# The FoX head beside each GDN head placed half a head later in a hybrid decoder step

## Chip, cores and metric

The kernel runs on one core of a Trainium2 chip. The metric is the device time of one execution in microseconds, as the median of three runs.

## What is computed

One layer of a hybrid decoder for 512 prompt tokens behind 16 meta tokens and for 8 sequences of 4 sampled tokens. A GDN group (gated delta rule, 8 heads) and a FoX group (softmax attention with a forget gate, 8 heads) run on one combined projection; a PEER layer, which looks up single neurons as experts, follows. Cut to what matters:

```python
xn = rmsnorm(h); p = xn @ w_in                      # columns: GDN q|k|v, a, b, z, FoX q|k|v, f, og
# GDN: conv + SiLU on q|k|v, L2 norm of q and k, then per chunk of tokens
rhs = beta * (v - exp(G) * (k @ S)); u = triangular_solve(a_strict, rhs)
o = exp(G) * (q @ S) + (qk * decay) @ u;  S = exp(G_last) * S + (k * tail).T @ u
gdn = rmsnorm(o) * silu(z)
# FoX: QK norm, causal softmax(q k / sqrt(128) + c_t - c_s) v; sampled tokens also see a paged cache
fox = rmsnorm(o_fox) * sigmoid(og)
h = h + concat(gdn, fox) @ w_out
# PEER: 8 heads x 16 experts of 16384 for each token
idx, gate = top16(product keys); hid = gelu(x . expert_u[idx]); h = h + sum(gate * hid * expert_v[idx])
```

## The kernel before

The 560 rows (32 sampled, 16 meta, 512 prompt) are worked in two groups: **a** has the first 256 rows (two tiles of 128, the sampled and meta rows in the first), **b** the other 304 (tiles of 128, 128 and 48). `front` runs for each group the stages norm and gates, `heads`, the output product, the norm before PEER, and the routing. Between two stages all engines meet at a barrier, and a stage's queue programs wait for its last stores before they get there. The experts of a group are gathered from memory (128 rows of 8 KB each by one indirect DMA from the POOL queue, into a ring of five buffers) and used by DVE, one item for each gather: a dot product (L1812) or a weighted sum (L1825). The gathers of group a begin with group b: in b's `heads` 330 items are placed between its own work (`quota`), and what is left runs at the end. Group a has no items.

`heads` is where the change lies. Each head pair needs eight segments of the projection, each 128 columns wide and 16 matmuls long (L795, `segment`, three or two PSUM buffers `pj`), with its 1 MB weight tile loaded by SP (L693); group a also stores each tile, packed, for group b (L1133). ACT takes a finished segment out of PSUM (`evacuations`, L1118 for the raw rows of GDN's q, k and v, L1124 for FoX's, L1127 for the gate z, L1130 for og).

The order of work on every engine is set by marks. The programs of GDN, FoX, projections, evacuations and items are generators that yield a number ahead of each step, and `Marks` always emits the step with the lowest number. A head is 100 marks long; GDN head h and FoX head h both begin at mark 100h, and the steps in them are at fixed distances (`at + 15` and so on). The projections are placed by

```python
G_Q, G_K, G_V, F_Q, F_K, F_V, G_Z, F_OG = range(8)

def segment_mark(j, step):
    return 12.5 * (j - 6) + 12.5 * step / KT
```

so six segments come ahead of mark 0 and the last ends at mark 725. Items stand at 100 * HEADS * (i + 0.5) / quota. An engine works strictly in this order; between engines, semaphores say when a result is there.

The steps of a GDN head that the text speaks of: at 2.5 DVE waits for the evacuated q, k, v rows (L1343); from 3 to 9 it does the convolution (L1356, L1358); at 12 SiLU (L1367); at 15 PE sums the squares (L844, L848); at 16 to 18.5 root and inverse on ACT, then the scaling on DVE (L1385); at 20 PE turns k (L859); from 28 to 76 six levels of the triangular solve go to and fro between PE and DVE (L886, L892, L896, L1413, L1417, L1421); from 77 to 97 one round for each tile carries the state S on; at 98 the output norm (ACT L1195, DVE L1462, L1463), at 98.6 PE turns it (L951), at 99 DVE writes mixT (L1467). In a the state of the sampled rows is stored by POOL at 98 (L1598), in b the final state by SP at 99 (L739). The steps of a FoX head: norms from 1 to 9 (L1025, L1038), in a the sampled rows against the cache from 9 to 37 (page transposes L967 with copies L1501 and L1234, products L985 and L1010), then the prompt blocks (scores L1063, exponential L1250, transposes L1080, products L1086, L1544), at 89 to 94 the output norm, its turn (L1095) and mixT (L1562).

## Time and profile before

| | us |
|---|---|
| three runs | 4745.6, 4751.4, 4766.0 (median 4751.4) |
| profiled execution, its own time | 4779.3 |
| its span | 4777.5 |
| busy: DVE, PE, POOL, ACT | 3371.8, 2412.1, 2363.8, 542.1 |
| `heads` of group a, first projection to last mixT | 68 to 936 |
| `heads` of group b, first projection to last mixT | 1351 to 2476 |
| bytes moved by DMA | 1515 MB, mean 317 GB/s |

PE is the matrix engine (PEld its weight loads), DVE the vector engine, ACT the scalar engine, POOL the one that issues the gathers, SP the one that issues the weight loads. Busy time is the time with an instruction in execution; the granted clock of PE is shown as a share of its full speed. "Idle before" is the time that an engine stood still ahead of a group of instructions, with what ended it. The `heads` stages of the two groups are read apart, since their limits differ.

### The profile page before, as it was taken

Reading aid. Unit: us, or ns where it says so; the run is one execution under the profiler, and the core shown is the slowest. Engines: PE = TensorE matmul, PEld = TensorE weight load, DVE = VectorE, ACT = ScalarE, POOL = GpSimd, SP = SyncE. Lnnn points to the kernel's source line nnn. Section 1 sums busy time; section 2 is a strip of 40 time slices with the busy share of each in tenths; the row PEclk is TensorE's granted clock in tenths of the full one; section 3 lists DMA queues with packets and bytes.
Section 4 is the critical chain, followed back from the end, with each engine's and each line's share of the span. In section 5 each row is a group of like instructions: output and inputs, shape, how many; then the busy total and the mean of one; then the engine's idle time right before and its main releaser. Section 6 shows DMA issues by size and latency. Waiting matters only on the chain. (4 is left out here: it accounts for less than half of the span.)

```text
span 4777.5 us, 35023 instructions
## 1 busy us (share of the span) xinstructions
PE 2412.1 (50%) x11665; PEld 1922.4 (40%) x11665; DVE 3371.8 (71%) x4421; ACT 542.1 (11%) x1305; POOL 2363.8 (49%) x1222
## 2 busy tenths in 40 slices
PE   5999999797388888888749465100000000000000
PEld 5888888686366666665537343100000000000000
DVE  1332333306748899988876678889988988979998
ACT  1222222201122222222210000000000000000000
POOL 1100000000125665656564312288887877878886
PEclk8988999798789999999859787555555555555555
DMA  6756666277659999999988855499999999999998
GB/s 181 216 175 197 196 204 190 74 279 242 220 195 413 393 396 394 393 380 392 343 345 350 326 219 202 147 397 420 404 393 394 422 390 409 422 369 421 408 421 354
DMA packets 444012, 1515.01 MB, mean 317 GB/s; under 512 B 42092, under 2 KB 276256, under 8 KB 277896
## 3 DMA queue, kind: packets, MB, share of 16 engines
q0 software_dynamic: 162080, 1160.16, 60.7%
q1 hardware_dynamic: 269080, 251.94, 16.9%
q10 hardware_dynamic: 12672, 100.67, 5.2%
q8 instruction: 93, 1.52, 0.1%
q14 instruction: 87, 0.71, 0.0%
HBM read 1384.96 MB, written 127.53 MB: 317 GB/s over the span
## 5 line engine op out<-in xcount | busy, mean ns | idle before, releaser
L1812 DVE CUSTOM_DVE_ANT_0 ex_ring<-ex_ring,ex_xi 128x2048 f32<-128x2048 f32 x544 | 1244.4, 2289 | 145.0 <-DMA ex_ring<-in_peer_u_dram,idx_all 77.2
L1825 DVE SCALAR_TENSOR_TENSOR ex_y<-ex_ring,ex_wt,ex_y 128x2048 f32<-128x2048 f32 x538 | 1264.4, 2350 | 113.9 <-DMA ex_ring<-in_peer_v_dram,idx_all 72.8
L1760 POOL DMA_INDIRECT ex_ring<-in_peer_u_dram,idx_all x384 | 790.2, 2058 | 342.8 <-DVE ex_hid L1812 135.1
L1760 POOL DMA_INDIRECT ex_ring<-in_peer_v_dram,idx_all x384 | 826.9, 2153 | 224.3 <-DVE ex_hid L1812 118.9
L795 PE MATMUL heads_b_pj<-xnT_b,heads_b_w 128*128 128x304 f32 x2048 | 608.0, 436 | 11.8 <-DMA heads_b_w<-w_scratch 8.5
L795 PE MATMUL heads_a_pj<-xnT_a,heads_a_w 128*128 128x256 f32 x2048 | 534.2, 401 | 20.5 <-DMA heads_a_w<-in_w_in_dram 20.5
L1760 POOL DMA_INDIRECT ex_ring<-in_peer_v_dram,ex_idx_s x160 | 310.7, 1942 | 328.8 <-DVE ex_hid L1812 156.6
L795 PEld LDWEIGHTS heads_b_pj<-xnT_b,heads_b_w 128*128 128x128 f32 x2048 | 380.5, 198 | 123.2 <-issue 15.3
L1760 POOL DMA_INDIRECT ex_ring<-in_peer_u_dram,ex_idx_s x160 | 320.6, 2004 | 207.9 <-DVE ex_y L1825 135.0
L795 PEld LDWEIGHTS heads_a_pj<-xnT_a,heads_a_w 128*128 128x128 f32 x2048 | 386.7, 201 | 72.4 <-DMA heads_a_w<-in_w_in_dram 21.1
L1592 POOL TENSOR_TENSOR heads_a_ub<-heads_a_uN,const 128x1024 f32<-128x1024 f32 x8 | 15.2, 1895 | 490.6 <-ACT heads_a_uN L1186 490.6
L1784 ACT ACTIVATE ex_act<-ex_hid 128x16 f32<-128x16 f32 x34 | 7.3, 215 | 1831.2 <-DVE ex_hid L1812 1831.1
L1756 POOL DMA_DIRECT2D ex_xi<-xi_scratch x13 | 6.9, 549 | 405.4 <-POOLq L249 330.5
L1892 PE MATMUL out_b_acc<-out_b_w,mixT_b 128*128 128x256 f32 (+1 forms) x768 | 170.3, 383 | 30.4 <-DMA out_b_w<-w_out_scratch 30.4
L1892 PEld LDWEIGHTS out_b_acc<-out_b_w,mixT_b 128*128 128x128 f32 (+1 forms) x768 | 128.8, 169 | 71.6 <-DMA out_b_w<-w_out_scratch 30.6
L2061 PE MATMUL route_b_pq<-mixT_b,route_b_w 128*128 128x304 f32 x512 | 143.0, 443 | 21.9 <-DMA route_b_w<-w_q_scratch 21.9
L2061 PEld LDWEIGHTS route_b_pq<-mixT_b,route_b_w 128*128 128x128 f32 x512 | 102.8, 203 | 60.8 <-DMA route_b_w<-w_q_scratch 22.1
L1892 PE MATMUL out_a_acc<-out_a_w,mixT_a 128*128 128x256 f32 x512 | 112.8, 384 | 25.9 <-DMA out_a_w<-in_w_out_dram 25.9
L2061 PE MATMUL route_a_pq<-mixT_a,route_a_w 128*128 128x256 f32 x512 | 114.6, 385 | 7.5 <-DMA route_a_w<-in_peer_w_query_dram 7.5
L1417 DVE TENSOR_TENSOR heads_a_yX<-heads_a_yX,heads_a_R 128x256 f32<-128x256 f32 x48 | 20.2, 421 | 136.0 <-PE heads_a_R L892 136.0
L1892 PEld LDWEIGHTS out_a_acc<-out_a_w,mixT_a 128*128 128x128 f32 x512 | 98.6, 193 | 39.9 <-DMA out_a_w<-in_w_out_dram 26.1
L2061 PEld LDWEIGHTS route_a_pq<-mixT_a,route_a_w 128*128 128x128 f32 x512 | 98.7, 194 | 21.4 <-DMA route_a_w<-in_peer_w_query_dram 7.9
(552 smaller groups left out, 3471.4 us busy)
## 6 DMA issues: line engine op xcount, KB each, us to landing
heads_a_w<-in_w_in_dram SPq DMA_DIRECT2D x64, 1024.0 KB, 6.1
w_scratch<-heads_a_w ACTq DMA_DIRECT2D x64, 1024.0 KB, 4.5
heads_b_w<-w_scratch SPq DMA_DIRECT2D x64, 1024.0 KB, 8.8
out_a_w<-in_w_out_dram SPq DMA_DIRECT2D x8, 2048.0 KB, 8.6
w_out_scratch<-out_a_w ACTq DMA_DIRECT2D x8, 2048.0 KB, 6.4
route_a_w<-in_peer_w_query_dram SPq DMA_DIRECT2D x16, 1024.0 KB, 7.1
w_q_scratch<-route_a_w ACTq DMA_DIRECT2D x16, 1024.0 KB, 6.7
out_b_w<-w_out_scratch SPq DMA_DIRECT2D x8, 2048.0 KB, 11.9
```

Of the source, the lines that this page charges most:

```text
L795: last = nc.tensor.matmul(pj[j % PJ][:, 0:N], B.w[:, j % W, k, :], xnT[:, k, :], start=(k == 0), stop=(k == KT - 1))
L1417: nc.vector.tensor_tensor(wide(B.XT), wide(B.XT), R1[:, 0:TW], ALU.subtract).then_inc(sem["XT_ready"], 1)
L1592: nc.gpsimd.tensor_tensor(B.ub[:], B.uN[:, 0, :].unsqueeze(1).to_broadcast([P, NB, HD]), cst("members", 0, NB).unsqueeze(2).to_broadcast([ ...
L1756: pool.dma_start(self.xi[part.on, :], self.xi_rows[part.xi_rows]).then_inc(self.sem["xi_in"], 16)
L1760: pool.indirect_dma_start(self.ring[:, i % RING, :], None, self.tables[which], bass.IndirectOffsetOnAxis(ap=self.index(s, g, k), axis=0)). ...
L1784: self.nc.scalar.activation(self.act[:, g % 2, :], self.hid[:, g % 2, :], ACT.Gelu).then_inc(self.sem["activated"], 1)
L1812: nc.vector.tensor_tensor_reduce(ring, ring, self.xi[:], 1.0, 0.0, ALU.mult, ALU.add, self.hid[:, g % 2, k:k + 1]).then_inc(self.sem["cons ...
L1825: nc.vector.scalar_tensor_tensor(y, ring, wt, y, ALU.mult, ALU.add).then_inc(self.sem["consumed"], 1)
L1892: last = nc.tensor.matmul(acc[0:b - a, i, 0:GW], mixT[:, k, a:b], w[:, c % 2, k, :], start=(k == 0), stop=(k == KT - 1))
L2061: last = nc.tensor.matmul(pq[s][:, 0:N], B.w[:, slot, k, :], xiT[:, k, :], start=(k == 0), stop=(k == KT - 1))
```

## The change

FoX head h begins at mark 100h + 50 instead of 100h, on all engines and in both groups. The segments are put in another order, z ahead of FoX's q, k and v, and all segments come three places later against the GDN heads: three of them ahead of mark 0 instead of six. The items of group b are spread over 850 marks instead of 800. The loads of the cache pages go with the FoX head.

```diff
-G_Q, G_K, G_V, F_Q, F_K, F_V, G_Z, F_OG = range(8)
-BASES = (0, C_K, C_V, C_FQ, C_FQ + HEADS * HD, C_FQ + 2 * HEADS * HD, C_Z, C_OG)
+G_Q, G_K, G_V, G_Z, F_Q, F_K, F_V, F_OG = range(8)
+BASES = (0, C_K, C_V, C_Z, C_FQ, C_FQ + HEADS * HD, C_FQ + 2 * HEADS * HD, C_OG)
...
 def segment_mark(j, step):
-    return 12.5 * (j - 6) + 12.5 * step / KT
+    return 12.5 * (j - 3) + 12.5 * step / KT
+
+
+def fox_mark(h):
+
+    return 100.0 * h + 50
...
-                            yield 100.0 * (h - 1) + step + 0.5 * i
+                            yield fox_mark(h - 1) + step + 0.5 * i
...
-                    at, n = 100.0 * h, h + 1
+                    at, n = fox_mark(h), h + 1
...
-                    at, n, qkv = 100.0 * h, h + 1, B.f_qkvT[:, h % 2]
+                    at, n, qkv = fox_mark(h), h + 1, B.f_qkvT[:, h % 2]
...
-                    yield 100.0 * HEADS * (i + 0.5) / quota
+                    yield (100.0 * HEADS + 50) * (i + 0.5) / quota
```

The new kernel's lines are five higher from here on (L795 is L800, L844 is L849, L1467 is L1472). What the marks make of it is seen in the order of the instructions. First PE in group a, early in a GDN head, from the transposes of the conv rows (L838, then L843) to the two sums of squares (L844 and L848, then L849 and L853). Before:

```order
L838 MATMUL heads_a_R<-const,heads_a_rowc 24x128 x3
L1030 MATMUL heads_a_F<-const,heads_a_f_qkvT 128x128 x2
L1032 MATMUL heads_a_F<-const,heads_a_f_qkvT 96x128
L795 MATMUL heads_a_pj<-xnT_a,heads_a_w 128x256 x2
L1038 MATMUL heads_a_F<-const,heads_a_f_qkvT 128x128 x2
L795 MATMUL heads_a_pj<-xnT_a,heads_a_w 128x256 x3
L967 MATMUL heads_a_F<-const,heads_a_kc 128x128 x8
L795 MATMUL heads_a_pj<-xnT_a,heads_a_w 128x256 x4
L967 MATMUL heads_a_F<-const,heads_a_kc 128x128 x8
L795 MATMUL heads_a_pj<-xnT_a,heads_a_w 128x256 x4
L844 MATMUL heads_a_R<-heads_a_qke,const 128x256
L848 MATMUL heads_a_R<-heads_a_qke,const 128x256
```

and now, on to the transposes of k (L864, before L859):

```order
L843 MATMUL heads_a_R<-const,heads_a_rowc 24x128 x3
L800 MATMUL heads_a_pj<-xnT_a,heads_a_w 128x256 x5
L1091 MATMUL heads_a_F<-heads_a_vM,heads_a_PT 128x128
L800 MATMUL heads_a_pj<-xnT_a,heads_a_w 128x256 x8
L849 MATMUL heads_a_R<-heads_a_qke,const 128x256
L853 MATMUL heads_a_R<-heads_a_qke,const 128x256
L800 MATMUL heads_a_pj<-xnT_a,heads_a_w 128x256 x2
L858 MATMUL heads_a_R<-const,heads_a_qkvT 128x128 x2
L800 MATMUL heads_a_pj<-xnT_a,heads_a_w 128x256 x4
L864 MATMUL heads_a_R<-const,heads_a_qkvT 128x128 x2
```

The projections are as many; the FoX matmuls between them have gone to the other half of the head, and one product of the FoX head before (L1091) stands there.

Second DVE at the end of group b's `heads`, from the last GDN head's mixT on. Before, the stage ended with it (the branches are the border of the stage):

```order
L1812 ISA ex_ring,ex_hid<-ex_ring,ex_xi 128x2048
L1812 ISA ex_hid 128x1
L1462 RECIPROCAL heads_b_ors<-heads_b_ort 128x3
L1463 TENSOR_TENSOR heads_b_gU<-heads_b_R,heads_b_ors 128x384
L1825 SCALAR_TENSOR_TENSOR ex_y<-ex_ring,ex_wt,ex_y 128x2048
L1467 SCALAR_TENSOR_TENSOR mixT_b<-heads_b_R,vecs,heads_b_gz 128x304
L679 UNCONDITIONAL_BRANCH
L1907 UNCONDITIONAL_BRANCH
```

and now 20 items follow, with the second half of the last FoX head between them; the first rows are:

```order
L1472 SCALAR_TENSOR_TENSOR mixT_b<-heads_b_R,vecs,heads_b_gz 128x304
L1817 ISA ex_ring,ex_hid<-ex_ring,ex_xi 128x2048
L1817 ISA ex_hid 128x1
L1830 SCALAR_TENSOR_TENSOR ex_y<-ex_ring,ex_wt,ex_y 128x2048
L1545 RECIPROCAL heads_b_rec<-heads_b_den 128x1
L1817 ISA ex_ring,ex_hid<-ex_ring,ex_xi 128x2048
L1817 ISA ex_hid 128x1
L1830 SCALAR_TENSOR_TENSOR ex_y<-ex_ring,ex_wt,ex_y 128x2048
```

The items there were taken out of the heads before, which now have fewer each.

## Rows read from the trace of the kernel before

**Rows 1.** Stretches: us, then busy us (instructions) per engine, granted clock, DMA share, GB/s

```profile
core 0: us, PE busy (x) PEld busy (x) DVE busy (x) ACT busy (x) POOL busy (x), PEclk, DMA share, GB/s
68.00:886.00 818.00, 799.54 (x4352) 693.85 (x4353) 253.79 (x734) 198.35 (x497) 77.00 (x86) 0.92 0.65 198
886.00:936.00 50.00, 41.03 (x194) 34.03 (x192) 17.21 (x45) 6.23 (x23) 2.84 (x2) 0.69 0.05 22
1360.00:1400.00 40.00, 40.00 (x158) 29.71 (x157) 4.75 (x9) 2.07 (x5) 0.93 (x1) 1.00 0.52 180
1535.00:2300.00 765.00, 651.09 (x3089) 474.92 (x3087) 693.72 (x767) 186.48 (x410) 479.11 (x238) 0.95 0.98 392
2388.00:2476.00 88.00, 47.60 (x196) 37.59 (x194) 85.23 (x87) 11.73 (x36) 71.42 (x31) 0.56 0.93 362
```

**Rows 2.** Waits of DVE, 1350 to 1534 us: total us, times, longest

```profile
DVE heads_b_rowc L1343 <- ACT heads_b_raw L1118: 21.9, 1, 21.9
```

**Rows 3.** Waits of PE in group a, 62 to 936 us

```profile
PE heads_a_F L967 <- DVE heads_a_kc L1501: 8.2, 8, 1.0
```

**Rows 4.** Timeline, third GDN head of group a: start us, us, engine, line, operation

```profile
321.86 0.44 PE L951 MATMUL heads_a_R<-const,heads_a_gU 128*128 128x128 f32 x2 [0.99 <-DVE heads_a_gU L1463]
...
324.67 1.27 DVE L1356 TENSOR_SCALAR heads_a_yX<-heads_a_raw,heads_a_tap 128x224 f32<-128x224 f32 x6
...
336.11 0.61 DVE L1358 SCALAR_TENSOR_TENSOR heads_a_yX<-heads_a_raw,heads_a_tap,heads_a_yX 128x224 f32<-128x224 f32 x2
...
339.59 0.59 PE L844 MATMUL heads_a_R<-heads_a_qke,const 128*128 128x256 f32 x2
...
343.91 0.69 DVE L1385 TENSOR_TENSOR heads_a_qkvT<-heads_a_qkvT,heads_a_th_root 128x512 f32<-128x512 f32 x1 [3.93 <-ACT heads_a_th_root L1167]
```

**Rows 5.** Groups of instructions by line: busy us, mean ns | idle before, releaser

```profile
L795 PE MATMUL heads_a_pj<-xnT_a,heads_a_w 128*128 128x256 f32 x2048 | 534.2, 401 | 20.5 <-DMA heads_a_w<-in_w_in_dram 20.5
L967 PE MATMUL heads_a_F<-const,heads_a_kc 128*128 128x128 f32 x128 | 18.3, 276 | 8.2 <-DVE heads_a_kc L1501 8.2
L1025 PE MATMUL heads_a_F<-heads_a_f_root,const 128*128 128x256 f32 x32 | 8.2, 379 | 0.0
L1358 DVE SCALAR_TENSOR_TENSOR heads_a_yX<-heads_a_raw,heads_a_tap,heads_a_yX 128x224 f32<-128x224 f32 (+1 forms) x144 | 53.7, 437 | 0.6
L1356 DVE TENSOR_SCALAR heads_a_yX<-heads_a_raw,heads_a_tap 128x224 f32<-128x224 f32 (+1 forms) x48 | 10.1, 283 | 0.0
```

**Rows 6.** A table load by line, and the root of a GDN head with its reader

```profile
L1140 ACT ACT_TABLE_LOAD x16 | 20.5, 1283 | 0.3
...
317.26 0.30 ACT L1195 ACTIVATE heads_a_ort<-heads_a_oms,const 128x2 f32<-128x2 f32 x1
...
321.19 0.16 DVE L1462 RECIPROCAL heads_a_ors<-heads_a_ort 128x2 f32<-128x2 f32 x1
```

**Rows 7.** The GDN heads' mixT, line L1467: ns min/median/max, first and last start

```profile
L1467 DVE SCALAR_TENSOR_TENSOR mixT_a<-heads_a_R,vecs,heads_a_gz x8: 483/484/485, 216.4 to 935.5; 128x256 f32<-128x256 f32 x8
L1467 DVE SCALAR_TENSOR_TENSOR mixT_b<-heads_b_R,vecs,heads_b_gz x8: 526/530/534, 1533.8 to 2475.2; 128x304 f32<-128x304 f32 x8
```

**Rows 8.** The items of the experts on DVE, groups by line

```profile
L1812 DVE CUSTOM_DVE_ANT_0 ex_ring<-ex_ring,ex_xi 128x2048 f32<-128x2048 f32 x544 | 1244.4, 2289 | 145.0 <-DMA ex_ring<-in_peer_u_dram,idx_all 77.2
L1825 DVE SCALAR_TENSOR_TENSOR ex_y<-ex_ring,ex_wt,ex_y 128x2048 f32<-128x2048 f32 x538 | 1264.4, 2350 | 113.9 <-DMA ex_ring<-in_peer_v_dram,idx_all 72.8
```

**Rows 9.** Timeline at the end of both `heads` stages

```profile
935.50 0.48 DVE L1467 SCALAR_TENSOR_TENSOR mixT_a<-heads_a_R,vecs,heads_a_gz 128x256 f32<-128x256 f32 x1 [0.53 <-PE heads_a_R L951]
945.76 0.33 SPq L1872 DMA_DIRECT2D hres_a<-in_x_sample_dram  x1
...
2475.16 0.53 DVE L1467 SCALAR_TENSOR_TENSOR mixT_b<-heads_b_R,vecs,heads_b_gz 128x304 f32<-128x304 f32 x1
...
2489.59 1.30 SPq L1872 DMA_DIRECT2D hres_b<-in_x_prompt_dram  x3
```

**Rows 10.** DMA issues: count, KB each, median us from issue to landing

```profile
out_gdn_sample_dram<-heads_a_sout POOLq DMA_DIRECT2D x8, 512.0 KB, 6.1
...
out_gdn_prompt_dram<-heads_b_S SPq DMA_DIRECT2D x8, 64.0 KB, 12.5
```

More of the change, by code:

```diff
@@ L1206, in fox @@
                 for h in range(HEADS):
-                    at, n, qkv = 100.0 * h, h + 1, B.f_qkvT[:, h % 2]
+                    at, n, qkv = fox_mark(h), h + 1, B.f_qkvT[:, h % 2]
                     yield at + 1
@@ L1284, in item_mark @@
             def item_mark(i):
-                return 100.0 * HEADS * (i + 0.5) / quota
+                return (100.0 * HEADS + 50) * (i + 0.5) / quota
             act.wait_ge(sem["f_cleared"], 5)
@@ L1483, in fox @@
                 for h in range(HEADS):
-                    at, n, qkv = 100.0 * h, h + 1, B.f_qkvT[:, h % 2]
+                    at, n, qkv = fox_mark(h), h + 1, B.f_qkvT[:, h % 2]
                     order = Counter(dve, sem["f_order"], n, 20)
@@ L1601, in fox @@
                 for h in range(HEADS):
-                    at, n = 100.0 * h, h + 1
+                    at, n = fox_mark(h), h + 1
                     yield at + 10
```

## The prediction

> **What bounds the kernel now.** I read the stage windows first, because the two groups have different limits. In group a (68 to 886 us) PE is busy 799.5 of 818 us while DVE is busy 254 and the DMA engines at 0.65 [rows 1]: PE alone sets the pace. After the last projection, from 886 to 936 us, PE is busy 41 of 50 us at a granted clock of 0.69, so 9 us are latency and part of the rest is the low clock. In group b, from 1535 to 2300 us, the DMA engines are at 0.98 and DVE busy 694 of 765 us, PE only 651 [rows 1]: the expert gathers and the DVE work on them set the pace. Just ahead, from 1360 to 1400 us, the reverse holds: PE projects without a gap at full clock, DVE has 4.8 us of work and the DMA engines stand at 0.52. That stretch is the lead in which six segments are projected before head 0 begins, and DVE spends 21.9 us of it waiting for the evacuated raw tile [rows 2]. The tail of b (2388 to 2476 us) is full again on DVE, 85 of 88 us.
>
> The sum is made against the profiled execution (4779.3 us, span 4777.5), 0.6% above the median of 4751.4; only its difference is carried over.
>
> **Group a, the lead and the work.** Three segments are projected ahead of head 0 instead of six. They are PE work either way and PE is the bound, so this term is 0. The same holds for the FoX head's instructions: as many, only later.
>
> **Group a, the new waits.** In each head PE waits about 1 us for the copied cache pages (L967), 8.2 us over eight heads [rows 3]. With FoX half a head later, DVE no longer has the convolution in front of the page copies, so I take the 8.2 us as gone (0 if not). Against that, FoX filled PE while the GDN head went through convolution and norms. Before, L951 starts at 321.86 us and L844, the first matmul that needs the convolved rows, at 339.59 [rows 4]: some 17.3 us from the end of one to the start of the other. Of these the page transposes (18.3/8 = 2.3 us), their wait (1.0) and the FoX sums (8.2/8 = 1.0) [rows 3, 5] move away, so PE will arrive after 13.0 us, at about 335.3. The convolution can start at 324.67 as now and takes 8.0 us when nothing of FoX stands in it ((53.7 + 10.1)/8 [rows 5]), to 332.7. From its last operation to L844 it was 339.59 - 336.72 = 2.9 us [rows 4], which gives 335.6: a wait of 0.3 us or a little more. The next is L859, which needs the normalised q and k: L1385 ends at 344.60, 5.0 us after L844 [rows 4], and in the new order only two sums, a transpose and six projection matmuls lie between. A projection matmul takes 0.43 us at full clock (40 us for 158 half records of 304 columns [rows 1], so 0.51 for one, scaled to 256 columns; the mean in group a, stretches at half clock among them, is 534.2/1024 = 0.52 [rows 5]). Nine matmuls at the first figure are 3.9 us. That is 1.1 us more. With the transpose in between I take 2.0 us a head, 16 us in all; the ends are 0 (the rows before it already show slack) and 5 us a head, 40 in all.
>
> **Group a, the end.** The last FoX head runs on alone for 45 marks: two transposes, copies, products, square, root, normalisation and turn, about ten handovers. By the same kind of steps in the old tail (9 us idle there for 75 marks) I take 9 us exposed, against which the old waits for the level products disappear because FoX's sampled part now stands between them: net +2. More of the tail's PE work lies in the stretch with no projections, where the clock was 0.69 [rows 1]: +3. Then the close of the stage gets shorter: the state store of the last GDN head lands about 6.1 us after its issue [rows 10], and the next stage began 9.8 us after the last mixT [rows 9]. That store will now be issued while the last FoX head still runs. I take 5 us off. Group a together: -8 + 16 + 5 - 5 = **+8 us**, ends -13 and +35.
>
> **ScalarE tables.** The new order has 15 more table loads: the GDN root needs one in each head (it had it free behind FoX's root), and the exponential after it another. Each takes 1.28 us [rows 6]. The root was ready at 317.56 and DVE came for it at 321.19 [rows 6], 3.6 us later, so one load is covered and the term is 0; without that cover it would be 16 x 1.28 = 20 us. The Trainium skill, "ScalarE: Activation LUTs", section "What ACT_TABLE_LOAD costs", gives about 2.66 us for each switch, drain included, and advises to batch by table set, which this change undoes; by the page the 3.6 us of cover would still just hold and the sum would stay the same, while without the cover it would be some 40 us. The trace shows 1.28 us and no more.
>
> **Group b, the lead.** 96 projections before, 48 now, at 158 records in 40 us [rows 1], two to a matmul: 96 records less, 24.3 us. If DVE sets the pace of the rest, all of it is saved (-24.3); if DMA does, only its idle share, 0.48 x 24.3 = -12.
>
> **Group b, the heads.** Seven heads took (2475.2 - 1533.8)/7 = 134.5 us each [rows 7]. The 330 items are now spread over 850 marks instead of 800, so 38.8 instead of 41.25 fall to a head. On DVE 2.4 items of (2289 + 2350)/2 = 2320 ns [rows 8] are 5.6 us; on the DMA engines 2.4 of 49.25 megabytes (gathers and eight weight tiles) are 4.9% or 6.6 us. Both point at about 129 us a head: 8 x 5.5 = **-44**. What was taken out comes back at the end: 20 items stand on DVE behind the last GDN head, 20 x 2.32 = 46 us, which cover the FoX chain entirely, since no handover there is longer than the two or three items between its steps. Its own DVE work was taken out of the first half head and comes with it; with DVE's short gaps I take **+47**. The close: the store of the last state takes 12.5 us to land behind the gathers [rows 10], and the next stage starts 13.9 us after the last mixT [rows 9]; it will be long done: **-7**.
>
> Group b: -24 - 44 + 47 - 7 = -28 by this count. By DMA time alone (same bytes, only the idle in the lead and at the close saved) it is -12 - 7 = -19. I take **-27**, nearer to the first, because DVE waits for DMA in few places. All stages behind run the same instructions, so it comes through. Sum: +8 - 27 = -19, and 4751 - 19 = **4732 us**.
>
> **Rivals.**
> *A. The b head does not get shorter (slower).* The GDN head is one chain through PE, ACT and DVE, and PE already waits in b. If that chain and not the items sets the 134.5 us, the 44 us do not come, while the 47 us of the half head at the end do: -24 + 0 + 47 - 7 = +16, and with the dearer end of group a's waits (+20) the kernel takes 4751 + 36 = 4787 us. For it: neither DVE nor the DMA engines are quite full. Against: PE's own load (651 of 765) leaves room. It decides from 134.5 - 28/8 = 131 us a head upwards; b then gains nothing.
> *B. DMA time is conserved.* Then b gives -19 us or less, a +8 to +16: 4742 to 4750, say 4747 us, no difference. For it: the DMA engines at 0.98; against: they rest for 25 us at the start of each head, where DVE is the bound.
> *C. No new waits in a, heads of b at 127.* The sampled attention, which now lies beside the GDN rounds, hides their latency better, and the convolution is clear of FoX. a gives -10, b -44: 4751 - 54 = 4697 us; taken as 4703.
> *That the change does something else than it says* can be left out: the order of instructions shows both groups shifted, with no instruction of PE or DVE added.
>
> **How the numbers follow.** A measurement of this kernel tells about 0.5% (24 us) from no change; the bound to "faster" is 4727.7 us. The forecast (4732, spreading from 4718 to 4744) has a chance of 0.48, half of it on either side of that bound; A 0.15, B 0.16, C 0.21. So faster 0.24 + 0.21 = 0.45, within 0.40 (0.24 + 0.16), slower 0.15. The range 4700 to 4770 reaches over C and B and the cheap part of A, and leaves about 0.2 out.
>
> **What the new profile would show.** Right: the lead of b about 24 us shorter, with DVE's wait for the raw tile nearly gone; the last mixT of the GDN heads in b at some 128 to 130 us from one to the next; DVE over 90% busy in the 50 us behind the last of them; the next stage starting 5 to 7 us after the last operation instead of 10 and 14; in a no wait on L967's line, and 1 to 2 us a head on the lines of L844 and L859. Wrong: a b head of 131 us or more (A), a head of group a longer than the present 102.7 us ((935.5 - 216.4)/7 [rows 7], the fast last one among them) by over 4 us (the end at 5 us of waits), or a lower granted clock in group a's steady heads, for which no row of before speaks, since the matmuls that it falls behind are the same.

## The result and the profile after

| | kernel before | changed kernel |
|---|---|---|
| time, median of 4 runs | 4758.7 us (4745.6 to 4779.6), 4751.4 before the fourth | 4700.5 us (4686.9 to 4714.6) |
| ratio | | 0.9874, 95% interval 0.9825 to 0.9922 |
| profiled execution, its span | 4779.3 us, 4777.5 | 4701.7 us, 4699.9 |
| group a, first projection to the first load of the next stage | 877.6 us | 833.2 us |
| group b, the same | 1138.8 us | 1108.2 us |

The changed kernel is 58 us (1.3%) faster; 19 were forecast. By the two profiles 44.4 us went in group a, where I had added 8, and 30.6 in group b, where I had taken off 27 (28 by the count of the terms). The other 2.6 of the 77.6 us between the spans lie outside the two stages, where the instructions are the same: 2.4 us more ahead of a, 3.5 more between a and b, 8.5 less behind b.

Group a first. Stretches of the changed kernel: us, then busy us (instructions) per engine, granted clock, DMA share, GB/s.

```profile
core 0: us, PE busy (x) PEld busy (x) DVE busy (x) ACT busy (x) POOL busy (x), PEclk, DMA share, GB/s
70.00:853.00 783.00, 766.43 (x4345) 667.38 (x4346) 249.98 (x745) 209.38 (x502) 76.75 (x86) 0.96 0.68 207
853.00:901.00 48.00, 39.84 (x201) 32.29 (x199) 12.40 (x32) 9.58 (x27) 2.84 (x2) 0.67 0.09 34
```

Beside [rows 1] this says where the time came from: PE is as full as before, does the same instructions in 34.3 us less busy time (766.43 + 39.84 against 799.54 + 41.03), and its granted clock over the long stretch is 0.96, not 0.92. In the kernel before it fell to half twice in every steady head. The same view of PE alone, 4 us at a time, in the third head; before:

```profile
core 0: us, PE busy (x), PEclk, DMA share, GB/s
344.00:348.00 4.00, 4.00 (x22) 0.52 0.55 153
348.00:352.00 4.00, 4.00 (x17) 0.50 0.00 0
352.00:356.00 4.00, 4.00 (x18) 0.70 0.00 0
356.00:360.00 4.00, 4.00 (x24) 1.00 0.40 164
360.00:364.00 4.00, 4.00 (x31) 1.00 0.54 165
364.00:368.00 4.00, 4.00 (x20) 0.58 1.12 296
368.00:372.00 4.00, 4.00 (x16) 0.56 0.43 112
```

and of the changed kernel:

```profile
348.00:352.00 4.00, 4.00 (x34) 1.00 0.52 151
352.00:356.00 4.00, 4.00 (x32) 0.77 0.64 177
356.00:360.00 4.00, 4.00 (x13) 0.50 0.02 4
360.00:364.00 4.00, 4.00 (x21) 0.88 0.00 0
...
372.00:376.00 4.00, 4.00 (x24) 0.83 0.80 199
376.00:380.00 4.00, 4.00 (x25) 0.74 0.00 0
```

0.50 is the lower of the two levels, 1.2 of 2.4 GHz. PE's busy time is 4.00 of 4.00 us in every row: the busy share shows nothing of it, the clock column does. What PE did before the clock fell is in its timeline, here of the kernel before:

```profile
342.21 1.93 PE L985 MATMUL heads_a_F<-heads_a_f_qkvT,heads_a_kc 128*128 128x4 f32 x16
...
345.12 3.55 PE L985 MATMUL heads_a_F<-heads_a_f_qkvT,heads_a_kc 128*128 128x4 f32 x16
...
349.07 3.78 PE L795 MATMUL heads_a_pj<-xnT_a,heads_a_w 128*128 128x256 f32 x8
...
362.02 4.62 PE L1010 MATMUL heads_a_F<-heads_a_sPT,heads_a_vc 128*128 128x4 f32 x32
```

These blocks are the products of the sampled rows with the cached pages, four columns each. The first 16 records take 1.93 us, the next 16 run into the low clock and take 3.55, and the eight projection records behind them 3.78 where 1.89 is usual.

Waits of PE in group a, changed kernel, 70 to 910 us (us in total, times, longest):

```profile
PE heads_a_R L956 <- DVE heads_a_gU L1468: 8.7, 8, 1.8
PE heads_a_R L864 <- DVE heads_a_qkvT L1390: 8.1, 8, 1.0
PE heads_a_F L1100 <- DVE heads_a_f_oN L1561: 3.5, 1, 3.5
```

The 8.2 us for the page copies [rows 3] are gone and 8.1 us at L864 (L859 before) have come: they cancel. Over the whole stage PE stands idle 26.9 us, 37.0 before, and is busy 34.3 us less; the two make up the 44.4.

Group b, changed kernel: 40 us of the lead, 840 us of steady heads, the half head at the end.

```profile
1312.00:1352.00 40.00, 39.71 (x166) 30.04 (x167) 17.26 (x35) 7.87 (x13) 2.89 (x3) 0.94 0.55 191
1460.00:2300.00 840.00, 730.91 (x3519) 529.78 (x3519) 764.74 (x870) 222.18 (x487) 492.56 (x257) 0.96 0.97 387
2357.00:2402.00 45.00, 7.58 (x32) 5.26 (x31) 43.19 (x36) 4.89 (x17) 35.12 (x17) 0.50 0.93 371
```

Lines that set mixT, first and last start, to hold against [rows 7]:

```profile
L1472 DVE SCALAR_TENSOR_TENSOR mixT_a<-heads_a_R,vecs,heads_a_gz x8: 483/484/486, 192.0 to 893.5; 128x256 f32<-128x256 f32 x8
...
L1472 DVE SCALAR_TENSOR_TENSOR mixT_b<-heads_b_R,vecs,heads_b_gz x8: 529/534/535, 1460.2 to 2357.3; 128x304 f32<-128x304 f32 x8
L1567 DVE SCALAR_TENSOR_TENSOR mixT_b<-heads_b_F,vecs,heads_b_gz x8: 533/534/534, 1520.5 to 2401.9; 128x304 f32<-128x304 f32 x8
```

Per GDN head of b that is (2357.3 - 1460.2)/7 = 128.2 us, 134.5 before. The first comes 147.9 us after the first projection, 183.0 before. The end of both stages, timeline:

```profile
893.53 0.48 DVE L1472 SCALAR_TENSOR_TENSOR mixT_a<-heads_a_R,vecs,heads_a_gz 128x256 f32<-128x256 f32 x1 [0.54 <-PE heads_a_R L956]
...
900.28 0.48 DVE L1567 SCALAR_TENSOR_TENSOR mixT_a<-heads_a_F,vecs,heads_a_gz 128x256 f32<-128x256 f32 x1 [0.58 <-PE heads_a_F L1100]
903.78 0.34 SPq L1877 DMA_DIRECT2D hres_a<-in_x_sample_dram  x1
...
2408.04 0.93 POOL L1765 DMA_INDIRECT ex_ring<-in_peer_u_dram,ex_idx_s  x1 [0.31 <-issue]
2420.50 1.31 SPq L1877 DMA_DIRECT2D hres_b<-in_x_prompt_dram  x3
```

The close of a stage is the time from its last operation to the start of the next stage. In a it is 3.0 us, 9.8 before [rows 9]. In b it is 13.6 us after the last item's operation (2406.9), as before (13.9).

### The profile page after: what moved, and what is told of

Read it like the earlier page. It is cut to its first block and busy times, and to the rows that moved or that the text cites. A ratio compares the mean times of both kernels' runs of the same rounds, so it can differ in the third digit from the quotient of the medians.

```text
span 4699.9 us, 35038 instructions
## 1 busy us (share of the span) xinstructions
PE 2368.1 (50%) x11665; PEld 1881.8 (40%) x11665; DVE 3365.4 (72%) x4421; ACT 566.0 (12%) x1320; POOL 2333.9 (50%) x1222
## 5 line engine op out<-in xcount | busy, mean ns | idle before, releaser
L1765 POOL DMA_INDIRECT ex_ring<-in_peer_v_dram,idx_all x384 | 801.1, 2086 | 240.9 <-DVE ex_hid L1817 136.9
L800 PE MATMUL heads_b_pj<-xnT_b,heads_b_w 128*128 128x304 f32 x2048 | 603.7, 433 | 11.2 <-DMA heads_b_w<-w_scratch 8.5
L800 PE MATMUL heads_a_pj<-xnT_a,heads_a_w 128*128 128x256 f32 x2048 | 526.9, 396 | 19.0 <-DMA heads_a_w<-in_w_in_dram 19.0
L800 PEld LDWEIGHTS heads_b_pj<-xnT_b,heads_b_w 128*128 128x128 f32 x2048 | 377.6, 197 | 121.7 <-issue 12.5
L1765 POOL DMA_INDIRECT ex_ring<-in_peer_u_dram,ex_idx_s x160 | 307.8, 1924 | 207.0 <-DVE ex_y L1830 138.4
L800 PEld LDWEIGHTS heads_a_pj<-xnT_a,heads_a_w 128*128 128x128 f32 x2048 | 381.6, 198 | 69.7 <-DMA heads_a_w<-in_w_in_dram 19.5
## 6 DMA issues: line engine op xcount, KB each, us to landing
out_b_w<-w_out_scratch SPq DMA_DIRECT2D x8, 2048.0 KB, 12.4
```

The source lines that it names most:

```text
L800: last = nc.tensor.matmul(pj[j % PJ][:, 0:N], B.w[:, j % W, k, :], xnT[:, k, :], start=(k == 0), stop=(k == KT - 1))
L1765: pool.indirect_dma_start(self.ring[:, i % RING, :], None, self.tables[which], bass.IndirectOffsetOnAxis(ap=self.index(s, g, k), axis=0)). ...
```

## The experiments

Theory 1: group a gained because less of it runs at half clock, and a microsecond at half clock costs half a microsecond. Theory 2: in b the work of DVE and the DMA engines is conserved, and what an edit saves is their idle time. In all kernels below the order of segments, the segments ahead of head 0, FoX's offset in marks and the marks over which b's items are spread are a row of a table for each group; the kernel before has (OLD, 6, 0, 800) and the changed one (NEW, 3, 50, 850) in both. Half clock time is taken from rows like those above, over the whole stage in steps of 4 us: twice the sum of 4 us x (1 - granted clock). Ratios are to the kernel before, timed alongside.

**e1, e2: one group at a time**

```diff
-PLANS = {"a": (OLD, 6, 0, 800), "b": (OLD, 6, 0, 800)}
+PLANS = {"a": (NEW, 3, 50, 850), "b": (OLD, 6, 0, 800)}   # e1
+PLANS = {"a": (OLD, 6, 0, 800), "b": (NEW, 3, 50, 850)}   # e2
```

> The change in group a alone; group b keeps its order, its six segments ahead and its FoX head beside the GDN head. Theory 1: what group a gained (its first projection to the start of the next stage, 868 + 10 us before and 830 + 3 us after) is the change's own work in a: about 35 of it in the heads, because each steady head has 6.8 us less at half clock, and 7 in the close. Then the total falls by 40 to 45 us against the kernel before and the span from 68 to the next stage is 833 +- 5 us again; the profile shows two half clock stretches a head that sum to about 10 us, not 17. Rival 1: the gain in a comes with the one chip or run that was profiled; then this kernel is within 10 us of the kernel before, or its profile shows 17 us a head at half clock again. Rival 2: group b needs a's shift for its own gain; excluded by the next run if that gives 35.

> The change in group b alone. Theory: lead 35 us shorter, seven steady heads at 128 us instead of 134.5, 45 us of FoX alone at the end, no saving in the close of the stage: 30 to 35 us less in b, 25 to 40 us less in all, nothing in group a (profile: 868 us from its first projection to its last operation, 17 us a head at half clock). Rival: b's gain rests on something that a's new order leaves behind (weights packed in another order); then below 15 us here.

e1: 4729.8 us, ratio 0.9916 (0.9889 to 0.9943); a 833.3 us with 99 at half clock, b 1133.8. e2: 4721.9 us, ratio 0.9897 (0.9866 to 0.9929); a 877.9 with 168, b 1111.0. Each group has its own gain without the other. The medians give 43 and 51 us, more together than both at once (58, beside a median of the kernel before that was 14 us lower); e2's runs are spread over 42 us, and its profiled execution, 4755.7, was the slowest. By stages the sum is right (44 and 28), though e2's 28 lies just under the 30 to 35 expected. In e1 b came out 5 us shorter with its code unchanged: so much must be allowed for b from one profile.

**e3: the items as before**

```diff
-PLANS["b"] = (NEW, 3, 50, 850)
+PLANS["b"] = (NEW, 3, 50, 800)
```

> The change in both groups, but the 330 expert items of group b spread over 800 marks as before instead of 850: as many items per GDN head as before, none beside the last half FoX head. If the items per head set the pace of a b head (my reading): the steady b head goes back to 133 to 135 us (+44 in all), the last half FoX head runs alone in 20 to 30 us instead of 45 (-15 to -25), so this kernel is 20 to 30 us slower than the changed one, that is 28 to 38 below the kernel before. If the FoX head's place sets it (two chains that no longer collide, so that a head is shorter whatever the items): the head stays at 128 to 130 us and this kernel is 15 to 25 us FASTER than the changed one.

4710.1 us, ratio 0.9870 (0.9843 to 0.9897): by the ratio not to be told from the changed kernel. In the profile b is 14.0 us longer (1122.2). The head is at 135.5 us, as my reading had it, but I had expected the whole kernel 20 to 30 us slower than the changed one, and it was 14 in the stage: the half head alone took 11.7 us instead of 44.6, cheaper than the 20 to 30 I had expected, and the close shrank to 2.0 us:

```profile
2418.50 0.53 DVE L1479 SCALAR_TENSOR_TENSOR mixT_b<-heads_b_R,vecs,heads_b_gz 128x304 f32<-128x304 f32 x1
...
2419.39 0.94 POOL L1772 DMA_INDIRECT ex_ring<-in_peer_u_dram,ex_idx_s  x1 [2.91 <-DVE ex_y L1837]
...
2430.20 0.53 DVE L1574 SCALAR_TENSOR_TENSOR mixT_b<-heads_b_F,vecs,heads_b_gz 128x304 f32<-128x304 f32 x1 [0.82 <-PE heads_b_F L1107]
2432.75 1.31 SPq L1884 DMA_DIRECT2D hres_b<-in_x_prompt_dram  x3
```

The last gather was issued at 2420.33, 12.4 us ahead of the next stage; in the changed kernel it is 11.5 us (2408.97 to 2420.50), with the last state stored at 2352.5, 68 us ahead. In the kernel before the last gather stands here, 12.3 us ahead of 2489.59:

```profile
2476.35 0.94 POOL L1760 DMA_INDIRECT ex_ring<-in_peer_u_dram,ex_idx_s  x1 [0.30 <-issue]
```

The close of b follows the last gather, not the store of the state. What of the gather the next stage waits for isn't seen.

**e4, e5: the small products spread between projections**

```diff
                     for b in range(NB):
+                        yield at + 17 + 1.75 * (1 - page) + 0.2 * b
...
                 for b in range(NB):
+                    yield at + 30 + 0.55 * b
                     for page in range(2):
```

> The kernel before, with one edit on TensorE's order in group a: the 16 and 32 matmuls of four columns with the cached pages (two blocks of 3.5 and 4.6 us) are given marks of their own over 3.5 and 4.4 marks, so that projection matmuls stand between them. As many instructions, no new wait. Before, the granted clock goes to half right behind each of these blocks, for 10.2 and 6.8 us in a steady head. Theory 1 (these blocks bring the half clock, and it costs half of the stretch that is PE's): most of the 17 us a head at half clock goes, a steady head falls from 105.8 to 98 to 101 us, the total by 35 to 60 us. Rival (the half clock comes from something else in these stretches, and the blocks only stand there; or it costs little): 105 us a head as before, total within 10 us. Rival (the small matmuls are dear wherever they stand): half clock stretches fall, but the head stays above 103 us.

4752.3 us, ratio 0.9967 (0.9948 to 0.9986): some 16 us by the ratio (7 to 25 by its interval), where I had expected 35 to 60. a 853.2 us with 116 at half clock: in four of six steady heads the stretch behind L1010 is gone, in two it is down to 3 or 4 us, and the one behind L985 is still there. That is one profile, of this kernel's fastest execution, and e10 will show that one profile can hold 53 us less half clock time than the next of the same kernel.

> The changed kernel with the same edit as e4: the four-column matmuls of the sampled attention in group a get marks of their own, with projections between them. In the changed kernel some 7 to 10 us a head are left at half clock (0.77, 0.50, 0.88 and 0.83, 0.74 over 4 us each in the head from 344 us on), and what stands ahead of the first block is dense. Theory 1 (the blocks bring the half clock, and each us of it costs half a us of PE): these stretches go for the most part, a steady head of a falls from 102.4 to 98 to 100 us, group a's stage from 833 to 808 to 822, the total by 10 to 25 us against the changed kernel (so 68 to 83 below the kernel before by its ratio 0.9874, 0.982 to 0.985). Rival (the change already had all there is to get, the rest of the half clock comes from other work): 833 +- 3 and no difference.

4699.8 us, ratio 0.9876 (0.9857 to 0.9896), the same as the changed kernel; a 839.0 with 115.5 at half clock, 6 us longer. A miss: spreading the blocks is no cure, and my idea of what keeps the clock up was too simple. Here too the stretch behind the second block went, in four of six steady heads, but the one behind the first is 10 us long, where the changed kernel has 7 and 3. One such head; the second block runs from 576.1 to 582.0:

```profile
557.00:561.00 4.00, 4.00 (x22) 0.60 0.57 159
561.00:565.00 4.00, 4.00 (x22) 0.50 0.02 4
565.00:569.00 4.00, 4.00 (x17) 0.62 0.00 0
...
577.00:581.00 4.00, 4.00 (x33) 1.00 1.14 292
```

What holds is the price, half of the half clock time.

**e6, e7: items in the lead**

```diff
-                return PLAN[0][3] * (i + 0.5) / quota
+                return -25 + 875 * (i + 0.5) / quota   # e6; e7: -25 + 860 * ...
```

> The changed kernel with the items of group b spread over marks -25 to 850 instead of 0 to 850: some 9 items stand in the lead, where VectorE is busy 17 of 40 us and the DMA engines stand at 0.55; 37.7 items instead of 38.8 a head. Theory 2 (in b VectorE's and the DMA engines' work is conserved, and what an edit saves is idle time of both): the first head comes later by 0 to 5 us, seven heads get shorter by 2 to 3 us each (1.1 items less), the stage falls from 1108 to 1088 to 1096, the total by 12 to 20 us against the changed kernel. Rival (the lead is a PE stretch and the ring of five buffers is empty there: the items only wait for their gathers): 1108 +- 4.

> As e6, but the items end at mark 835 instead of 850. The close of b (last mixT operation to the next stage) was 14 us in the changed kernel and 2.0 us with the items ending at mark 800; in three kernels the next stage starts 11.5 to 12.4 us after the last gather was issued. Theory (the last gather's landing sets the close, and the FoX head's last steps can run beside it): the close falls from 14 to 3 to 8 us, the stage is 3 to 8 us shorter than in e6. Rival (the FoX chain, then alone, comes as much later): same as e6 within 3 us.

e6: 4681.5 us, ratio 0.9842 (0.9823 to 0.9861), b 1089.4, the head 125.9. e7: 4679.7 us, ratio 0.9837 (0.9821 to 0.9853), b 1088.0. Theory 2 holds: the lead's first 20 us had 4.9 us of DVE work in the changed kernel and have 17.0 now, with the DMA engines at 0.99 in the second half. e7's own expectation was missed: its last mixT stands 9.1 us ahead of the next stage instead of 18.0 in e6, but the heads took back what it saved (126.9 us instead of 125.9, seven times), with the DMA engines at 0.97. Its last gather, issued at 2382.90, is again 12.3 us ahead of the next stage, though the last operation is not:

```profile
2381.96 0.94 POOL L1772 DMA_INDIRECT ex_ring<-in_peer_u_dram,ex_idx_s  x1 [0.31 <-issue]
2385.58 0.53 DVE L1574 SCALAR_TENSOR_TENSOR mixT_b<-heads_b_F,vecs,heads_b_gz 128x304 f32<-128x304 f32 x1 [0.82 <-PE heads_b_F L1107]
2395.18 1.31 SPq L1884 DMA_DIRECT2D hres_b<-in_x_prompt_dram  x3
```

**e8, e11: FoX 60 and 45 marks behind, in group a**

```diff
-PLANS["a"] = (NEW, 3, 50, 850)
+PLANS["a"] = (NEW, 3, 60, 850)   # e8; e11: 45
```

> The changed kernel with FoX 60 marks instead of 50 behind the GDN head in group a (group b as changed). If group a's gain is the clock of two stretches, it depends on what stands beside the sampled products and not on the half head as such: the half clock time of a steady head differs from the changed kernel's 7 to 10 us, and the length of the head moves by half of that difference (102.4 us if as much, 98 if none, 106 if 17). Behind the last GDN head 10 marks more of FoX alone: +2 to +5 us. Rival (a gains because the two chains stand apart, so that PE waits less): PE's waits in a, 16 us in all in the changed kernel, change by more than 5 us and the head with them, the half clock time not.

4713.9 us, ratio 0.9908 (0.9890 to 0.9926). a 839.1 us, 105 at half clock; behind the last GDN head 13.6 us instead of 10.3. Half clock time and head (100.7 us, 100.2 in the changed kernel) stayed alike, and PE's idle time is 29.2 us for 26.9, so the rival isn't borne out. The profiled execution is this kernel's second fastest.

> The changed kernel with FoX 45 marks behind the GDN head in group a (group b as changed). By the relation found so far: stage = half of the half clock time + 782 us (order of the change), less 2 to 3 us for five marks less of FoX alone behind the last GDN head. At 60 marks the half clock time was 105 us, at 50 marks 99 to 108. If the time at half clock depends on the neighbours of the sampled products, anything from 60 to 140 us can come, and the stage has to be 779 + half of it within 3 us; if the half head as such is what matters, it is 95 to 110 us again and the stage 827 to 834.

4731.1 us, ratio 0.9938 (0.9917 to 0.9959). a 858.2 with 124 at half clock: the constant is 796.0, not 779, so the stage is 17 us longer than by that relation. PE's idle time is 36.7 us where the changed kernel has 26.9:

```profile
PE heads_a_F L1042 <- ACT heads_a_f_qkvT L1136: 6.1, 8, 0.8
PE heads_a_F L1092 <- ACT heads_a_Pb L1262: 4.4, 7, 0.6
```

L1042 is the turn of FoX's v, whose segment is evacuated at mark 50 when three segments are ahead: 45 is too early for it. So the offset is tied to the lead.

**e9: the small products left out, but for those of the last of eight batch rows**

```diff
-                    for b in range(NB):
+                    for b in range(NB - 1, NB):   # in both loops
```

> The kernel before; of the matmuls of four columns in group a (16 a head against the cached keys, 16 against the cached values) only those of the last batch row stand (2 and 2). The scores and outputs of the sampled rows lack the other seven: that part is left out. At full clock the blocks take about 3.9 and 4.6 us a head, so 7.7 us a head or 62 in all go with them as such. In nine runs the stage of group a is half of its half clock time plus a constant (794 us in the order of before, 167.6 us at half clock). Theory 1 (these blocks bring the half clock of the steady heads): of the 168 us some 130 go too, the stage falls from 878 to 745 to 765 us. Rival (other work brings it, and the blocks only stand there): 168 us at half clock stay, the stage falls to 812 to 820.

4666.7 us in one run; a 760.1 us, 19.5 at half clock. The outputs of the sampled rows lack what is left out. The rival is out: of the 117.5 us by which the stage is shorter, 74 are half of the half clock time that went, and 43 the work itself, where I had put 62. PE, two of five stretches of 100 us that all show the same clock, kernel before:

```profile
300.00:400.00 100.00, 97.76 (x538) 0.91 0.62 192
400.00:500.00 100.00, 97.77 (x537) 0.91 0.62 187
```

e9:

```profile
300.00:400.00 100.00, 97.59 (x568) 1.00 0.73 223
400.00:500.00 100.00, 96.74 (x556) 1.00 0.76 231
```

**e10 and what was open: the second half of the page transposes 1.5 marks later, and profiles repeated**

```diff
-                        yield at + 12.5
+                        yield at + 14
```

> The kernel before with one mark changed: the third and fourth set of page transposes in group a stand at 14 instead of 12.5, which puts two projection matmuls more ahead of them and of PE's wait for the page copies (1.03 us a head, the only idle time of PE in the 8 us ahead of the first block of sampled products). Theory (that wait, which the change also took away, is why the kernel before falls to half clock two matmul groups earlier and for longer, 10.2 us against 6.8): the wait shrinks to 0 to 0.3 us and the half clock behind the first block from 10.2 to about 7 us; the stage falls by 6 us for the waits and by 8 to 14 for the clock, 878 to 858 to 864. Rival (only the blocks and what stands behind them count): the wait goes, the half clock time stays at 165 to 170 us, the stage is 870 to 873.

The wait for the page copies fell from 8.2 to 1.3 us; 3.3 came at L844's line and 2.1 at L853's. So the rest of the stage (its length less half of its half clock time) is no shorter. a 854.0 us with 117 at half clock: for the clock as expected, it seemed. But the median is 4771.5 us (4748.7 to 4791.8), ratio 1.0022 (1.0001 to 1.0043). The profiled execution was at 4749 one of its two fastest. So the same kernels were profiled again: the kernel before (o1 to o3), e10's (o4), and last the changed kernel and e7's (c1, c2).

> The kernel before, instruction for instruction, profiled again. If half clock time in group a varies between executions (theory 3): it lies anywhere between 100 and 170 us, the stage is 794 + half of it, and the total follows: 4779 with 168, 4765 with 140, 4750 with 110. If it is a property of the program: 165 to 170 us and a stage of 876 to 879 us at any total, and what varies lies in group b and behind it.

> As o1, a second time: the profiles of this kernel together have to lie on one line (stage = 794 + half of the half clock time) under theory 3, or in one point (877 us, 168 us) under its rival.

> As o1, a third time, with the same two outcomes: a point on the line 794 + half of the half clock time somewhere between 845 and 880 us, or the one point of 877 and 168 us.

> The kernel of e10 profiled again. Its 12 executions lay between 4749 and 4792 us, the profiled one at 4749 with a stage of 854.0 us. Theory 3: a longer stage of 860 to 890 us if this execution is one of the slower ones, the wait for the page copies 1.3 us as before, the stage again a constant plus half of the half clock time (the constant some 8 us below 794, since the waits of 8 us are gone). Rival: 854 +- 2 again, whatever the total.

> The changed kernel, instruction for instruction, profiled and timed again. Theory 3 with the change keeping its heads out of the long pattern: 97 to 110 us at half clock in group a, stage 831 to 837, b 1106 to 1114, median 0.985 to 0.990 of the kernel before, and a narrower spread of its executions than that of the kernel before (under 25 us, against 47). Rival (the changed kernel has long patterns too and was lucky in five profiles): more than 115 us at half clock, stage 840 or more.

> The kernel of e7 (changed kernel, items of group b over marks -25 to 835) once more, now in one call with the changed kernel. In b 18 to 22 us less than c1 (1088 against 1108), group a the same: 15 to 25 us below c1 by the medians, 0.981 to 0.986 of the kernel before. Rival (what is saved in b is lost behind it, because each expert item that is not taken there is taken later): within 5 us of c1. The number of items taken in b is the same in both, so I hold the first.

All profiles of group a, "rest" being the stage less half of the half clock time:

| kernel | its time, us | stage a | half clock | rest |
|---|---|---|---|---|
| before | 4779.3 | 877.6 | 167.6 | 793.8 |
| o1, the same | 4780.1 | 878.7 | 165.1 | 796.1 |
| o2, the same | 4754.9 | 863.5 | 139.9 | 793.5 |
| o3, the same | 4781.3 | 874.1 | 160.7 | 793.7 |
| e2 | 4755.7 | 877.9 | 168.0 | 793.9 |
| e4 | 4742.9 | 853.2 | 116.1 | 795.2 |
| e10 | 4749.4 | 854.0 | 116.9 | 795.6 |
| o4, the same | 4781.1 | 879.6 | 169.6 | 794.8 |
| changed | 4701.7 | 833.2 | 102.6 | 781.9 |
| c1, the same | 4687.9 | 831.6 | 97.5 | 782.8 |
| e1 | 4727.0 | 833.3 | 99.2 | 783.7 |
| e3 | 4713.1 | 834.7 | 108.0 | 780.7 |
| e6 | 4686.9 | 833.1 | 98.9 | 783.7 |
| e7; c2, the same | 4683.2; 4672.0 | 833.2; 833.1 | 102.8; 99.0 | 781.8; 783.6 |
| e5 | 4711.0 | 839.0 | 115.5 | 781.3 |
| e8 | 4702.2 | 839.1 | 104.8 | 786.7 |
| e11 | 4748.6 | 858.2 | 124.4 | 796.0 |
| e9 | 4666.7 | 760.1 | 19.5 | 750.4 |

The rest is a property of the order, the half clock time in part one of the execution. o4 shows it hardest: one mark's change had "saved" 24 us of the stage in one profile and cost 2 in the next. In o2 even the heads of one execution differ:

```profile
300.00:400.00 100.00, 97.59 (x565) 0.97 0.67 206
400.00:500.00 100.00, 97.70 (x533) 0.91 0.62 187
...
700.00:800.00 100.00, 97.77 (x556) 0.95 0.65 200
```

The order of the changed kernel's group a was profiled seven times (changed, c1, e1, e3, e6, e7, c2) and always lay at 98 to 108 us. c1 and c2, timed side by side: 4700.8 us, ratio 0.9879 (0.9854 to 0.9904), and 4684.3 us, 0.9841 (0.9816 to 0.9865), with b 1107.6 and 1088.4. The kernel of e7 is 17 us faster than the changed kernel by these medians. c1's runs lay over 34 us, more than the 25 I had allowed.

## Why the prediction was wrong

**Group a, the waits.** That L967's 8 us go was right, and the kind of wait that takes their place too; its size was not. I had counted 0.3 us at L844, nothing came there, and 1.1 at L859, where 1.0 came, and then "took" 2.0 us a head with the transpose in between. It is 8.1 us where I put 16: what was worked out from [rows 4, 5] was better than the allowance laid on top.

**Group a, the end and the close.** Predicted +5 for the half head alone and -5 for the close. The last FoX head ends 6.8 us after the last GDN head, 9 were taken, and the next stage starts 6.8 us sooner after the last operation. But the last GDN head, too, now comes sooner behind the last projection, so the tail from the end of the projections to the last operation is 2.1 us shorter (49.5 to 47.4), where I had +5; of those, 3 were for the clock, and the tail's half clock time is the same (30.7 and 31.1 us). The close gave 6.8 where I had 5.

The stretch from the first to the last projection is 35.5 us shorter (818.3 to 782.8). Its half clock time fell from 129.2 to 68.3 us, which is worth 30.5; the waits of PE that I had counted cancel (-8.2 and +8.1), and for the last 5 us, of which 2.3 are idle time of PE, the profiles name no single cause. So without the clock the stage is some 14 us shorter, half of it the close, and my terms without the clock give +5. (The "rest" of the table moves by 11.9, since it counts half clock time of an idle PE too.)

**Group a, the clock: the step that failed.** The prediction held a lower clock in the steady heads for something of which "no row of before speaks, since the matmuls that it falls behind are the same", and gave the clock no term there. The matmuls are the same, their neighbours are not. In profiles of the kernel before 140 to 168 us of the stage are at half clock, in those of the changed kernel 98 to 103: 19 to 35 us of time. That is the term that was put at nothing, and by the first two profiles (32 us) it is larger than the whole forecast. It was no unknown size: [rows 1] has the clock of 0.92 over 818 us, 65 us of loss in a stage whose bound is PE, and I read only the busy time beside it. The question to ask was what those 65 us hang on, and both bounds of the range should have had them, a gain as well as a loss.

The Trainium skill, "TensorE: Matmul & The Clock Gate", section "Terms", puts the price of throttled time at that time multiplied by the part of the pulses left out. The table agrees at half: from 116 to 170 us at half clock, 27 us of stage, the rest of the old order moves by 3.

**ScalarE's tables: right.** The loads are there (144 for 129, at 1283 ns; in the third head of a the work on ACT ends at 306.87 and goes on at 308.19 with a load between) and PE's wait behind the GDN root is the 8.7 us that it was. The loads of that root:

```profile
L1200 ACT ACT_TABLE_LOAD x16 | 20.5, 1283 | 0.3
```

**Group b, the lead: right in size, wrong in its row.** The first head comes 35.1 us sooner; the lead and one head's items were to give 24.3 + 5.5 = 29.8. But DVE's wait for the raw tile [rows 2] is not "nearly gone": it is 22.2 us. What went is the wait that stood beside it in the view of before and that I hadn't taken up, DVE behind FoX's root:

```profile
DVE heads_b_f_qkvT L1489 <- ACT heads_b_f_root L1219: 27.5, 1, 27.5
DVE heads_b_rowc L1343 <- ACT heads_b_raw L1118: 21.9, 1, 21.9
```

**Group b, the heads: right.** 128.2 us, predicted about 129, and e3 shows the cause: with the items back at 41 a head it is 135.5. **The end:** 44.6 us of FoX alone with items, +47 predicted, DVE busy 43 of 45. **The close: wrong.** The 7 us for the store of the state did not come. The stage ends 11.5 to 12.4 us after the last gather, in e2, e6 and e7 too (12.3, 11.5 and 12.3; of all profiles only o4 has more, 13.5), and the items, which I had moved to the very end, keep that last gather there. [Rows 9, 10] held the store beside the close, and I took company for cause. e7 shows that to move it alone gives next to nothing. By the profile's rows b is -35 us for the lead and first head, -44 for seven heads, +49 from the last GDN head to the last item and 0 for the close; by my terms -30, -38, +47 and -7. That the sum is near is in part luck: 11 us too little taken off in front stand against 10 us too much hoped for at the end.

**The rivals.** A (the head does not get shorter) and B (DMA time conserved, 19 us or less in b) are out. B leaned on a misreading too: it had the DMA engines resting for 25 us at the start of each head, and in the kernel before they are at 1.02 from 1535 to 1560 us, with one dip to 0.43 in the 5 us behind; and from its own terms (-19, +8 to +16) follow 4740 to 4748 us, not 4742 to 4750. C's time was nearly right, 4697 us, by luck: it had b at -44, which was -31, and a at -10 for want of new waits, where new waits came (8.1 us) and the close went instead. Neither it nor any case had the clock. The ends of a's term, -13 and +35, don't follow from the bounds beside them either; those give -8 to +40.

**What stays open.** What the matmuls around a block must be like for the clock to stay up: e4 and e5 made the same edit; in both the stretch behind the second block went in most heads, and in e5 the first one grew by as much. Why the changed order settles near 100 us in every profile while the one before wanders. And the share of the clock in the measured 58 us: by the means of their profiles (four of before, two of the change) a gained 41 us and b 30, 72 in all, where the two timings say 60 and 58 by their ratios, with intervals of 37 to 83 and 46 to 70, and 58 and 69 by their medians. Counting the experiments, nine profiles of b's old plan lie at 1132 to 1143 us and six of its new one at 1108 to 1115; the means are 25 us apart, and so part of the 30 is scatter. Three of the four profiled executions of the kernel before were slower than its medians beside the experiments (4759 to 4773). That the unprofiled, faster ones spent less time at half clock fits the mean granted clocks of 58 timed executions of the kernel before (the ten fastest 0.739 to 0.746, the ten slowest 0.732 to 0.740) but was not seen stretch by stretch.

## What to carry to other kernels

Where PE is the bound, read its clock beside its busy time, 4 us at a time over one head: busy microseconds at half clock are bought at twice their price, and an edit that only changes neighbours can give them back. A single profile doesn't tell the gain of such an edit: profile the same kernel again before a cause is named, and hold the stage's length less half of its half clock time against the other kernel's; here it was steady within 3 us for one order. Where DVE and DMA are the bound, look for the idle time in the lead of a stage and put the streamed work there, and ask for every close which transfer it really waits for.

## What the runs showed of the hardware

PE can be busy 4.00 of 4.00 us and be granted 1.2 GHz of 2.4, behind blocks of matmuls of four columns: with those left out the clock stayed at 1.00 from 300 to 800 us, 19.5 us at half clock for 168. The same program on the same inputs had 117 and 170 us at half clock in two executions. And b's `heads` ended 11.5 to 12.4 us after its last gather was issued in 18 of 19 profiles (13.5 in o4), whether the last state had been stored 7 us before that gather (the kernel before) or 56 us (the changed one).
